# Moving every large on-chip tile of a fused transformer program to a multiple of 2048 bytes

## The reference

```python
for l in range(2):                                              # first_block
    x = x + 0.5 * swiglu_ffn(x, ffn1_norm[l], ffn1_w_gate[l], ffn1_w_up[l], ffn1_w_down[l])
    h = rms_norm(x, mix_norm[l])
    aq, ak, av, bq, bk, bv, cq, ck, cv, cg, gates = jnp.split(h @ w_in[l], ...)
    y_a = diff_attention(...); y_b = chunk_attention(...); y_c = retention(...)
    merged = g[0] * (y_a @ w_branch_a[l]) + g[1] * (y_b @ w_branch_b[l]) + g[2] * (y_c @ w_branch_c[l])
    x = x + merged @ w_out[l]
    x = x + 0.5 * swiglu_ffn(x, ffn2_norm[l], ffn2_w_gate[l], ffn2_w_up[l], ffn2_w_down[l])
# second_block, one layer
x = x + concatenate([dilated_attention, ssd_mixer, rglru_mixer]) @ w_out
x = x + (silu(h @ w_gate) * (h @ w_up)) @ w_down               # h = rmsnorm(x)
out = rmsnorm(x, norm_final)
```

## The kernel before

| tiles | first byte | address modulo 2048 |
|---|---|---|
| `x`, `xh`, `xl`, `raw`, `wh`, `wl`, `const`, and in their place `xwh`, `xwl`, `s1`, `s3`, `s4` | 4224 (`x`) to 90240 (`const`) | 128 |
| `vec`, `sm`, `sm2`, `sm3`, `eps`, `neg` (small) | 96384 to 123328 | various |
| `acc`, `r`, `sc` | 98720, 100768, 102816 | 416 |
| from `phase` on: `G*` (`Ga`, `gn`, `gnf`), `uh`, `ul`, `uf`, `s2`, `xraw`, the mixers' tiles | 123392 (`phase`) to 225792 | 512 |

## Time and profile before

### The profile page before, as it was taken

How to read it: one execution, slowest core, us unless ns; L and a number is a source line. 1 busy time by engine, 2 the same in 40 slices (tenths; PEclk the granted TensorE clock), 3 DMA queues, 4 the chain that set the end, 5 groups by cost and what they waited for, 6 DMA issues and landing times.

```text
span 3244.1 us, 39004 instructions
## 1 busy us (share of the span) xinstructions
PE 3198.3 (99%) x15098; PEld 2587.7 (80%) x15098; DVE 2088.9 (64%) x3338; ACT 1453.6 (45%) x2271; POOL 75.9 (2%) x153
## 2 busy tenths in 40 slices
PE   9999999999999999999999999999999999999998
PEld 7888877777787888788977777877889877878887
DVE  7333587745467657757688764557576677877656
ACT  5222456534244435534455653235353465354433
POOL 0000020100000000000010100000000100000000
PEclk9999999999999999999999999999999999999999
DMA  4322332322233234233232222341331545133231
GB/s 150 98 93 93 94 114 62 102 85 83 93 124 117 69 97 130 69 101 106 61 107 78 88 88 78 98 150 61 96 118 54 106 76 84 63 124 117 71 95 56
DMA packets 244553, 304.10 MB, mean 94 GB/s; under 512 B 11664, under 2 KB 198416, under 8 KB 244368
## 3 DMA queue, kind: packets, MB, share of 16 engines
q1 hardware_dynamic: 237616, 284.73, 29.3%
q0 software_dynamic: 6608, 16.79, 1.8%
q10 hardware_dynamic: 144, 0.10, 0.0%
HBM read 293.17 MB, written 2.10 MB: 91 GB/s over the span
## 4 chain that ended last, share of the span: by engine, by line
PE 88%; DVE 7%; ACT 3%; issue 1%; DMA 0%; DVEq 0%; ACTq 0%
PE bank L221 85%; PE bank L227 2%; DVE k_sc L183 1%; DVE k_wl L173 1%; ACT k_sc L217 1%; DVE k_sc L173 1%; ACT k_wh L217 1%; DVE k_x L183 0%; DVE k_acc L173 0%; DMA k_raw<-in_ffn_w_gate 0%; ACT L211 0%; DVE k_s L173 0%; DVE k_ul L183 0%; ACT k_uh L217 0%; DVE k_xraw L173 0%
## 5 line engine op out<-in xcount | busy, mean ns | idle before, releaser
L173 DVE TENSOR_TENSOR k_wl<-k_raw,k_wh 128x1024 fp32r<-128x1024 f32 (+2 forms) x354 | 417.4, 1181 | 499.4 <-ACT k_wh L217 481.2
L217 ACT ACTIVATE k_wh<-k_raw 128x1024 fp32r<-128x1024 f32 (+2 forms) x354 | 360.3, 1022 | 516.5 <-PE bank L221 392.3
L221 PE MATMUL bank<-k_xh,k_wh 128*128 128x512 f32 x1096 | 454.6, 415 | 3.8 <-ACT k_sc L217 1.5
L221 PE MATMUL bank<-k_xh,k_wl 128*128 128x512 f32 x1096 | 428.2, 391 | 0.1
L221 PE MATMUL bank<-k_xl,k_wh 128*128 128x512 f32 x1096 | 427.5, 390 | 0.0
L217 ACT ACTIVATE k_wh<-k_xraw 128x1024 fp32r<-128x1024 f32 (+1 forms) x230 | 228.2, 992 | 389.5 <-PE bank L221 316.1
L173 DVE TENSOR_TENSOR k_wl<-k_xraw,k_wh 128x1024 fp32r<-128x1024 f32 (+1 forms) x230 | 261.8, 1139 | 199.4 <-ACT k_wh L217 181.2
L221 PE MATMUL bank<-k_wh,k_s 128*128 128x512 f32 (+1 forms) x1040 | 306.3, 375 | 0.4 <-ACT k_sc L217 0.4
L221 PE MATMUL bank<-k_wh,k_uf 128*128 128x512 f32 (+1 forms) x1000 | 299.0, 380 | 1.0 <-DVE k_sc L183 1.0
L221 PE MATMUL bank<-k_gn,k_wh 128*128 128x512 f32 x840 | 264.5, 396 | 0.0
L221 PEld LDWEIGHTS bank<-k_xh,k_wh 128*128 128x128 f32 x1096 | 206.4, 188 | 64.1 <-issue 18.8
(11 more groups left out here) (385 smaller groups left out, 5981.2 us busy)
## 6 DMA issues: line engine op xcount, KB each, us to landing
k_raw<-in_w_in SPq DMA_DIRECT2D x153, 512.0 KB, 3.5
k_xraw<-in_ffn_w_down SPq DMA_DIRECT2D x40, 512.0 KB, 5.1
k_xraw<-in_ffn_w_gate SPq DMA_DIRECT2D x39, 512.0 KB, 3.7
k_raw<-in_ffn_w_up SPq DMA_DIRECT2D x37, 512.0 KB, 3.7
k_xraw<-in_ffn_w_up SPq DMA_DIRECT2D x33, 512.0 KB, 4.0
k_raw<-in_ffn_w_gate SPq DMA_DIRECT2D x29, 512.0 KB, 3.6
k_raw<-in_ffn_w_down SPq DMA_DIRECT2D x28, 512.0 KB, 3.5
k_raw<-in_w_out SPq DMA_DIRECT2D x28, 512.0 KB, 3.4
```

What stands on the lines that cost most here:

```text
L173: return q.op(lambda e: e.tensor_tensor(out, a, b, op), cost(out))
L217: return self.A.op(lambda e: e.activation(out, a, f, bias=bias, scale=scale), c)
L221: fn = lambda e: e.matmul(out, l, r, start=start, stop=stop, skip_group_check=True)
```

## The change

The change gives the same tiles other addresses. No instruction is added, removed or moved on any engine: the order of the instructions on PE, DVE, ACT, POOL and SP is the same in both programs, but for line numbers and the numbers in tiles' names.

```diff
@@ __init__
-        self.off = (nc.sbuf_base + 63) // 64 * 64
+        self.base = (nc.sbuf_base + 2047) // 2048 * 2048
@@ build
+        self.off = (self.nc.sbuf_base + 63) // 64 * 64
+        sm = self.sb("sm", 64)
+        sm2 = self.sb("sm2", 16)
+        sm3 = self.sb("sm3", 312)
+        epst = self.sb("eps", 2)
+        negt = self.sb("neg", 16)
+        assert self.off <= self.base
+        self.off = self.base
         Xt = self.sb("x", 8 * T)
         self.off_xh = self.off
...
         C = self.sb("const", NCONST)
-        Vv = self.sb("vec", NVEC)
-        sm = self.sb("sm", 64)
-        sm2 = self.sb("sm2", 16)
-        sm3 = self.sb("sm3", 312)
         ACCt = self.sb("acc", T)
         Rt = self.sb("r", T)
         SCt = self.sb("sc", NSC * T)
-        epst = self.sb("eps", 2)
-        negt = self.sb("neg", 16)
-        self.phase = (self.off + 63) // 64 * 64
+        self.phase = self.base + (self.off - self.base + 2047) // 2048 * 2048
+        Vv = self.sb("vec", NVEC, at=self.phase + 102 * 1024)
```

## The result

The changed kernel takes 3213.19 us, the median of 4 runs (3208.39 to 3215.72), against 3242.09 us of the kernel before (4 runs, 3241.82 to 3246.01). The ratio is 0.9906, with a 95% interval from 0.9889 to 0.9923. The profiled execution took 3214.16 us, its span 3212.4.

The account below looks back on a forecast made before the run. TensorE's matmuls were taken as the bound: 41 us at 80% is 33, less 5% for waits 31, plus 1 is 32; 3242.19 - 32 = 3210 us. Range 3198 to 3248, some 82%.

Parts of the forecast that it names:

- two seams: Kernel before: `linear` from `xh`, `xl` to `Ga`, 226.7 to 233.3 ns; `ffn_blocks` from `s4` to `s2`, 226 to 232.
- The region: Rival, 20%: a stream is slower when one operand lies in the upper part of the addresses; nothing changes, 3242 us.
- The multiple of 512: Rival, 15%: an operand beginning at 0 modulo 512 is itself slow; the kernel gets slower, 3267 us.
- moving operand in the last group, 4656: Matmuls streaming `Ga`, `gn`, `gnf`, `uh`, `ul` and the mixers' tiles: 6.6 ns saved each, 30.7 us.
- `uf`, `s2` stationary, 512 columns, 1728: Feed-forward matmuls of four layers with weights moving past `uf` or `s2`: 5 ns saved each, 8.6 us.
- `uf`, `s2` stationary, 384 columns, 768: The feed-forward matmuls of 384 columns past `uf` or `s2`: 2.6 ns saved each, 2.0 us.
- these three, with restarts: The three matmul terms, 41 us, taken at 80% because matmuls after a stall aren't in steady stream: 33 us.
- pairs that were equal before ("seams"): Matmuls at the start of stretches, where no seams between kinds remain: 1 us of gain.
- waits: Where TensorE waits for VectorE and ScalarE it would only wait longer: 5% taken off, 33 to 31 us.
- The two deductions: On the matmul gain: 80% for restarts after stalls, then 5% off for waits; without both, 3200 us.
- its third rival: VectorE's results come too late everywhere, so waits halve the gain: 3226 us, inside the forecast's range, no separate chance.
- the seam gone: Sign, in the feed-forward layers: the step in matmul time from `s4` to `s2` must vanish in the changed kernel.

Follow-up runs that it names:

- p128: Changed kernel with every tile of the last group 128 bytes higher, the first group left in place; 3243.74 us, ratio 0.9997 to the kernel before.
- all128: Changed kernel with every large tile, first and last group alike, 128 bytes higher; 3213.07 us, ratio 0.9903 to the kernel before.
- min256: Kernel before with only two roundings changed from 64 to 256 bytes, order of tiles kept; 3212.30 us, ratio 0.9903 to the kernel before.
- p256: Changed kernel with every tile of the last group 256 bytes higher; 3212.83 us, ratio 0.9902 to the kernel before.
- p64: Changed kernel with every tile of the last group 64 bytes higher; 3229.58 us, ratio 0.9956 to the kernel before.
- p192: Changed kernel with every tile of the last group 192 bytes higher; 3238.90 us, ratio 0.9982 to the kernel before.
- p32: Changed kernel with every tile of the last group 32 bytes higher; 3244.22 us, ratio 1.0000 to the kernel before.
- p96: Changed kernel with every tile of the last group 96 bytes higher; 3244.57 us, ratio 1.0001 to the kernel before.

## Why the prediction was right

**The mechanism.** The prediction had it from two seams in one trace: a pair that begins at the same place is fast. p128, all128 and min256 show it apart from everything else that the change does. Both rivals are dead. The region: `Ga` at the changed kernel's 122880, far above `wh`, streams at 226.6 ns. The multiple of 512: with every operand on one, nothing got slower, and with all of them off it (all128) nothing got faster. The Trainium skill's rule of two independent read ports ("SBUF — State Buffer", "Who interferes with whom") would have left the time at 3242. The measurements speak against what the prediction drew from it: the ports may be two, but the step of a matmul depends on the addresses of both operands, 226.6 against 233.3 ns.

What the text had wrong is the modulus. It said 512 where 256 is enough (p256, min256). Its "whichever of the two it is that lies otherwise" holds at 128 bytes, the only unequal distance in the kernel before, since 128 ahead and 128 behind are the same modulo 256; at 64 bytes it doesn't hold (p64, p192). No number of the forecast hung on either, since the change makes the places equal.

**The sum.** I took the distance from each matmul to the next in both traces, matched one to one (they are the same 15098), and added up the differences by kind; a distance of 260 ns or more in either trace counts as a wait.

| term | predicted, steady stream | measured |
|---|---|---|
| moving operand in the last group, 4656 | 30.7 | 26.0 |
| `uf`, `s2` stationary, 512 columns, 1728 | 8.6 | 8.4 |
| `uf`, `s2` stationary, 384 columns, 768 | 2.0 | 1.8 |
| these three, with restarts | 41 x 80% = 33 | 36.2 |
| pairs that were equal before ("seams") | 1 | 1.1 |
| waits | -5% of 33 = -2 | -5.7 |
| sum | 32 | 31.6 |

The windows of stationary `uf` and of `Ga` were sound prices: `Ga` gave 6.6 ns a step, `gn` 6.2, `uf` 5.0 with 512 columns. The two deductions were chosen, and both were mis-sized, in opposite directions. The stream gave 88% of its upper end, not 80%: of the 4656 steps of the first row only 146 are 260 ns or longer in either trace, and only a small group of the mixers is far under the price (`ya` 1.8 ns a step). The waits took 16% of what the stream gave, not 5%. They grew in many places by some tenths of a us (the fences of waits above), which the prediction named as its third rival in a stronger form. That it is no accident of one trace, the pages of the other runs show: TensorE stood still for 50.0, 51.9 and 51.8 us in p256, all128 and min256 (span less busy time), and for 44.5, 45.8, 43.9 and 46.7 in p128, p32, p96 and p192. That the two wrong deductions cancel, so that 32 stands beside 31.6, is luck.

Where the gain comes in follows the count of dearer steps. By the start of the same matmul in both traces, the changed kernel is 3.1 us ahead at 500 us of the kernel before, 3.4 at 800, 16.3 at 1800 and 16.4 at 2000: in the mixers hardly anything differed, so nothing is won. Between 900 and 1600, in two feed-forward layers, it wins 10.4.

**From span to median.** The sum gave 3214 us for the profiled execution and 3212 for its span; 3214.16 and 3212.4 were measured. The median came out at 3213.19 and not at 3210, because the prediction took along the 3.75 us by which the profiled execution of before lay above its median, and that of the changed kernel lies 1.0 above. Beside the experiments, with 13 and 19 runs of the kernel before, its median is 3244.3 to 3244.6, and the layouts with equal places lie 31 to 32 us under it, which is the sum.

**What should have shown it.** `Ga` at 227, the seam gone, 384 columns at 173, the splits at 1224 and 1223 ns, the transfers at 3.7 us: all as named.

## What to carry to other kernels

If a stream of float32r matmuls, each with a weight load of its own, is the bound, divide the length of steady windows by their weight loads, kind by kind; kinds with the same shape and the same clock that differ by 2 or 3% may differ in where their two operands begin. Give the moving and the stationary tiles the same address modulo 256 bytes (rounding each group up to 256 is enough, round addresses beyond that bring nothing), and expect 5 to 6.6 ns in a steady stream for each step of 512 columns whose places were 128 apart. Other types, and matmuls that keep their weights, were not measured here. A sum made from steady streams is an upper end: here the stream gave 88% of it, and 16% of that went into waits on engines that hadn't become faster.

## What was not expected of the hardware

- The price doesn't rise with the distance: 32 bytes cost all of it (233.3 ns), 64 cost a third (228.9), 96 all of it again.
- It has a direction. Moving 64 bytes ahead of stationary, modulo 256, costs 2.3 ns a step; 64 behind costs 6.7, whichever of the two was moved (p64, p192). The other unequal places of the table lie between 232.2 and 234.1; with one window for each, no order among them is shown.
- With 384 columns it goes otherwise. By the median distance of two starts, steps past `uf` and `s2` took 175 to 176 ns in the kernel before, p64 and p128 (moving minus stationary 128 and 192), but 173 in p32, p96 and p192 (224, 160, 64), where no price was left. No run here tells why, nor why the step depends on the two addresses at all.
- Even an equal pair needs 226.4 to 226.7 ns. No layout tried here went under that.
